# Ends of two feed-forward blocks reordered, and two half outputs of the next stage made before the stage boundary

## The chip, the cores and the metric

The kernel runs on one core of a Trainium2 chip. The metric is the device time of one execution in microseconds (us), taken as the median of several runs. The engines of the core work beside each other and wait for one another through semaphores: TensorE (PE in the rows: matmuls and transposes), VectorE (DVE), ScalarE (ACT), GpSimd (POOL), and SyncE (SP), which here issues the DMAs. A row "PE clock" gives the TensorE clock that was granted, as a share of its full 2.4 GHz; 0.50 is the lower of its two levels, 1.2 GHz.

## The reference

The computation is a two-layer encoder on 1024 tokens of width 1024, in float32. Layer 0 mixes with an S5 state space, layer 1 with an HGRN2 recurrence; after each mixer and after each feed-forward part a residual is added and a layer norm taken.

```python
def swiglu(x, w_in, w_out):
    gate, up = jnp.split(x @ w_in, 2, axis=-1)
    return (jax.nn.silu(gate) * up) @ w_out

def hgrn2_mixer(x, w_in, lower_bound, norm_g, w_out):
    q, f_fw, f_bw, i_in, g = jnp.split(x @ w_in, 5, axis=-1)   # width 1024 each
    ...                                   # q = silu(q); gates from f_fw, f_bw; 8 heads of 128
    o = rms_norm(o, norm_g) * jax.nn.silu(g)
    return o @ w_out

for layer in range(2):
    m = s5_mixer(h, ...) if layer == 0 else hgrn2_mixer(h, ...)
    h = layer_norm(ALPHA * h + m, ln_mix_g[layer], ln_mix_b[layer])
    f = swiglu(h, ffn_w_in[layer], ffn_w_out[layer])
    h = layer_norm(ALPHA * h + f, ln_ffn_g[layer], ln_ffn_b[layer])
```

## The kernel before, in words

The program is a row of stages, each an instruction block with a barrier of all engines at its end: S5, then `project_and_feed` (tiles named s5o), then the HGRN (tiles named hg), then `project_and_feed` again (tiles named hgo). The order of the instructions on each engine is the order in which each engine's own code is written; there is no scheduler. Each engine runs its list in order, and a wait at the head of the list holds up everything behind it.

**Numbers as pairs.** A float32 product is made of three matmuls of rounded parts: hi times hi, hi times lo, lo times hi. ScalarE makes a hi part (`split_hi`, line 62), VectorE or GpSimd subtracts it to get the lo part. The activations, with the width on the partitions, are `x_hi` and `x_lo` (tiles aT_hi, aT_lo).

**The feed-forward part.** The hidden width of 2816 is 22 chunks of 128, taken in 11 groups of two. For each group the two chunks are made, and `outputs` (lines 513 to 527) multiplies them with the group's rows of w_out: 16 products m = 0..15, two halves of the width for each of the eight token tiles, six matmuls each, into PSUM banks 4 + m % 4. VectorE adds each into h (`accumulate`, line 894). Bank m % 4 is free for product m + 4 once that is done (semaphore out_acc).

**The end of the last group (LAST), which the change touches.** The last chunk is made in a plain way in two token halves: `last_unit(0)` (four `plain_part`s of twelve matmuls, line 488, banks 0 and 1) and `last_unit(1)` (banks 2 and 3). Each half then passes ScalarE (silu), VectorE (`half_product`, line 875), ScalarE (hi) and GpSimd (`hidden_lo`, line 1023, semaphore hid) before `outputs` may use it. Tiles 0 to 3 need only half 0, tiles 4 to 7 need half 1. On TensorE the order is: last_unit(0), outputs of tiles 0 to 3, last_unit(1), transposes of tiles 0 to 3 (`turn_last`, line 411), outputs of tiles 4 to 7, transposes of tiles 4 to 7. The transposes put the normalised tokens into `x_hi` and `x_lo` for the HGRN, so they are there only in the first of the two blocks (`turns`); they go through the same banks 4 to 7, two banks a tile, and ScalarE and VectorE (`keep_turned`, line 831) empty them. After the second block the normalised rows go to the output.

VectorE takes the tiles in pairs. For each pair: `accumulate` with statistics (lines 894 and 897, two instructions for each product), then `normalise`: a chain of thirteen tiny instructions (lines 787 to 801) and four passes over 1024 columns (lines 805 and 808). `half_product` of half 1 stands behind pairs 0 and 1, then come keep_turned of tiles 0 to 3, then pairs 2 and 3, then keep_turned of tiles 4 to 7.

**The start of the HGRN.** For each head five outputs o = 0..4 (q, two forget gates, input, output gate) are made in two token halves: `unit(m, o, half)`, 24 matmuls at line 2112, into bank `half`. For head 0 all ten stand at the front of TensorE's list. A unit may overwrite its bank only when the result before it is read: unit (1, half) waits for q_kept, units (2, half) for f_kept. ScalarE starts with two small sigmoids of a table that depends on four DMAs of constants issued at the start of the stage, and only then takes the sigmoid of q (line 2246); VectorE then multiplies it (`keep_q`, line 2364). The weights of o = 0 and 1 of head 0 were already loaded and split in the block in front (w_raw, w_hi, w_lo); those of o = 2 are loaded at the start of the stage and split there when the units of o = 0, which share their buffer, are done.

## Time and profile before

| | us |
|---|---|
| median of 3 runs | 2784.15 |
| lowest, highest | 2781.75, 2785.19 |
| the profiled execution | 2782.6 |
| its span in the trace | 2780.8 |

TensorE is busy for 2562.8 us of that span, VectorE for 1831.1, GpSimd for 827.1, ScalarE for 813.5. The mean granted clock of TensorE is 0.959. The s5o block ends, and the HGRN begins, at about 1249.8 us of the span; the hgo block ends the program at 2780.8.

In a row of the timeline the first number is the start in us, the second the time from there to the end of the merged instructions, then engine, line, operation, what is written and read, the count, and in brackets the time the engine was idle before it and what ended that. One matmul of 512 columns shows about 0.39 us although the next starts sooner, since they overlap in the engine: the distance between starts is what counts.

### The profile page before, as it was taken

How to read it: one execution, taken by the hardware profiler on the slowest of the kernel's cores; microseconds unless marked ns; L12 is line 12 of the kernel's file. 1: busy time of each engine (PE TensorE's matmuls, PEld its weight loads, DVE VectorE, ACT ScalarE, POOL GpSimd, SP SyncE). 2: the span in 40 equal slices, each digit the busy share in tenths (PEclk: the TensorE clock that was granted, in tenths of full speed). 3: DMA queues.
4: the chain of work that ended last, by engine and by line, in shares of the span. 5: the costliest groups of instructions: out<-in, count | busy, mean ns of one | idle time of the engine just before them, and what ended most of it. 6: DMA issues, size and time to landing. Idle time of an engine off the chain costs nothing. (4 is left out here: it accounts for less than half of the span.)

```text
span 2780.8 us, 40502 instructions
## 1 busy us (share of the span) xinstructions
PE 2562.8 (92%) x13124; PEld 2148.0 (77%) x13124; DVE 1831.1 (66%) x3173; ACT 813.5 (29%) x1379; POOL 827.1 (30%) x606
## 2 busy tenths in 40 slices
PE   6787799999999999968999999997899999999995
PEld 5676577778888888757888888886687888888884
DVE  8789618666666666582667666667676666666657
ACT  3223323433332323312222323221233233323220
POOL 2968410433332323401111111110034333333240
PEclk9888899999999999989999999998899999999997
DMA  4333214134434434312010111000413444344341
GB/s 135 92 100 100 81 29 166 54 99 137 126 114 116 132 106 136 114 62 59 23 39 23 38 30 38 23 23 0 167 42 103 123 134 121 113 122 127 106 129 61
DMA packets 388063, 246.16 MB, mean 89 GB/s; under 512 B 23936, under 2 KB 370176, under 8 KB 387072
## 3 DMA queue, kind: packets, MB, share of 16 engines
q1 hardware_dynamic: 387968, 244.92, 29.5%
q8 instruction: 56, 0.92, 0.1%
q14 instruction: 39, 0.32, 0.0%
HBM read 227.10 MB, written 17.76 MB: 88 GB/s over the span
## 5 line engine op out<-in xcount | busy, mean ns | idle before, releaser
L894 DVE TENSOR_TENSOR h<-h,ps 128x512 f32<-128x512 f32 x320 | 219.1, 686 | 157.2 <-PE ps L525 157.0
L2112 PE MATMUL ps<-aT_hi,w_hi 128*128 128x512 f32 x640 | 257.1, 402 | 1.8 <-PEq L322 1.8
L2084 POOL TENSOR_TENSOR w_lo<-w_raw_plain,w_hi 128x1024 fp32r<-128x1024 f32 x38 | 91.8, 2423 | 560.1 <-ACT w_hi L62 560.1
L2112 PE MATMUL ps<-aT_hi,w_lo 128*128 128x512 f32 x640 | 251.5, 393 | 0.0
L2112 PE MATMUL ps<-aT_lo,w_hi 128*128 128x512 f32 x640 | 250.2, 391 | 0.0
L996 POOL TENSOR_TENSOR s5o_w_sets_plain<-s5o_w_sets_plain 128x512 f32<-128x512 f32 x100 | 137.4, 1379 | 223.8 <-DMA s5o_w_sets_plain<-in_ffn_w_in_dram 223.8
L476 PE MATMUL ps<-aT_hi,s5o_w_sets 128*128 128x512 f32 x640 | 203.0, 393 | 0.0
L476 PE MATMUL ps<-aT_hi,hgo_w_sets 128*128 128x512 f32 x640 | 202.8, 393 | 0.0
L996 POOL TENSOR_TENSOR hgo_w_sets_plain<-hgo_w_sets_plain 128x512 f32<-128x512 f32 x100 | 136.2, 1366 | 222.5 <-DMA hgo_w_sets_plain<-in_ffn_w_in_dram 222.4
L525 PE MATMUL ps<-hgo_w_hi,hgo_hid_hi 128*128 128x512 f32 x352 | 138.9, 395 | 11.6 <-POOL hgo_hid_lo L1023 11.6
L62 ACT ACTIVATE s5o_w_sets<-s5o_w_sets_plain 128x512 fp32r<-128x512 f32 x152 | 92.6, 627 | 178.7 <-POOL s5o_w_sets_plain L996 157.1
L62 ACT ACTIVATE hgo_w_sets<-hgo_w_sets_plain 128x512 fp32r<-128x512 f32 x152 | 92.7, 627 | 176.1 <-POOL hgo_w_sets_plain L996 155.9
L525 PE MATMUL ps<-s5o_w_hi,s5o_hid_hi 128*128 128x512 f32 x352 | 137.7, 391 | 5.1 <-POOL s5o_hid_lo L1023 3.4
L476 PEld LDWEIGHTS ps<-aT_hi,s5o_w_sets 128*128 128x128 f32 x640 | 120.5, 188 | 26.4
L2112 PEld LDWEIGHTS ps<-aT_hi,w_lo 128*128 128x128 f32 x640 | 120.3, 188 | 26.3
L476 PEld LDWEIGHTS ps<-aT_hi,hgo_w_sets 128*128 128x128 f32 x640 | 120.2, 188 | 26.3
L2112 PEld LDWEIGHTS ps<-aT_hi,w_hi 128*128 128x128 f32 x640 | 120.7, 189 | 25.0 <-issue 2.0
L2112 PEld LDWEIGHTS ps<-aT_lo,w_hi 128*128 128x128 f32 x640 | 120.6, 189 | 24.4
L525 PE MATMUL ps<-hgo_w_lo,hgo_hid_hi 128*128 128x512 f32 x352 | 138.4, 393 | 0.0
L525 PE MATMUL ps<-hgo_w_hi,hgo_hid_lo 128*128 128x512 f32 x352 | 138.4, 393 | 0.0
L525 PE MATMUL ps<-s5o_w_hi,s5o_hid_lo 128*128 128x512 f32 x352 | 137.7, 391 | 0.0
L525 PE MATMUL ps<-s5o_w_lo,s5o_hid_hi 128*128 128x512 f32 x352 | 137.6, 391 | 0.0
(380 smaller groups left out, 6332.3 us busy)
## 6 DMA issues: line engine op xcount, KB each, us to landing
s5o_w_sets_plain<-in_ffn_w_in_dram SPq DMA_DIRECT2D x208, 256.0 KB, 3.3
hgo_w_sets_plain<-in_ffn_w_in_dram SPq DMA_DIRECT2D x208, 256.0 KB, 3.3
w_raw_plain<-in_hg_w_in_dram SPq DMA_DIRECT2D x40, 512.0 KB, 4.0
s5o_w_sets_plain<-in_ffn_w_in_dram SPq DMA_DIRECT2D x96, 128.0 KB, 2.6
hgo_w_sets_plain<-in_ffn_w_in_dram SPq DMA_DIRECT2D x96, 128.0 KB, 2.7
s5o_w_lo_plain<-in_ffn_w_out_dram SPq DMA_DIRECT2D x11, 1024.0 KB, 5.0
hgo_w_lo_plain<-in_ffn_w_out_dram SPq DMA_DIRECT2D x11, 1024.0 KB, 5.0
h<-in_x_dram SPq DMA_DIRECT2D x4, 1024.0 KB, 8.9
```

What stands on the lines that cost most here:

```text
L62: return eng.activation(hi, src, ACT.Copy)
L476: ins = t.matmul(ps[:, to, :], w[:, kk, :], x_sets[x][xs][:, kk, :], start=(kk == 0 and m == 0), stop=(kk == 3 and m == 2))
L525: ins = t.matmul(ps[:, 4 + m % 4, :], x[:, q, tt * P:(tt + 1) * P], w[:, q, dh * HALF:(dh + 1) * HALF], start=(q == 0 and n == 0), stop=(q ...
L894: v.tensor_tensor(to, to, ps[:, 4 + m % 4, :], ALU.add).then_inc(S["out_acc"], 1)
L996: g.tensor_tensor(other, one, other, PRODUCTS[r][2]).then_inc(S["set_sum"], 1)
L2084: g.tensor_tensor(w_lo[b][:, :, :], w_raw[b][:, :, :], w_hi[b][:, :, :].bitcast(F32), ALU.subtract).then_inc(E[f"w_lo_done{b}"], 1)
L2112: ins = t.matmul(ps[:, half, :], w[b][:, kk, :], x[:, kk, cols], start=(kk == 0 and q == 0), stop=(kk == KT - 1 and q == 2))
```

## The change

Four things change.

1. On TensorE, in both feed-forward blocks, the first plain part of half 1 moves in front of the outputs of tiles 0 to 2, the other three stand behind them, and the outputs of tile 3 follow. The parts of half 1 wait for just the weight sets they need.
2. Tiles 4 to 7 are made in two pairs, each with the transposes of an earlier pair in front of it: transposes of 0 and 1, outputs of 4 and 5, transposes of 2 and 3, outputs of 6 and 7. The waits follow: a transpose of tile n waits until its two banks have been accumulated, and the outputs of tile t wait only for keep_turned of tile t - 4.
3. On VectorE `normalise` is cut in two (`moments`, the chain of tiny instructions, and `scale`, the four passes), half_product of half 1 moves in front of the scaling of pair 1, and keep_turned of tiles 2 and 3 stands between moments and scale of pair 2.
4. `next_units`: the units (0, half 0) and (1, half 0) of head 0 of the HGRN, 48 matmuls on the columns of tokens 0 to 511, are issued at the end of the s5o block, between the outputs of tiles 6 and 7 and the transposes of tiles 4 to 7, into banks 0 and 2. The HGRN's TensorE list starts with unit (0, half 1), then (1, half 1) and on; ScalarE reads the result of (1, half 0) from bank 2 and no longer waits for the two units that are there from the start.

```diff
@@ turn_last @@
                 t.wait_ge(S["normed"], NT + n + 1)
-                if n >= 2:
+                if n < 6:
+                    t.wait_ge(S["out_acc"], LAST * NOUT + 2 * (n + 3))
+                else:
                     t.wait_ge(S["hi"], NT + 2 * (n - 1))
                     t.wait_ge(S["lo"], NT + 2 * (n - 1))
@@ plain_part @@
-                t.wait_ge(S["plain_lo"], 6 * last + (n + 1 if half == 0 else 6))
+                t.wait_ge(S["plain_lo"], 6 * last + (n + 1 if half == 0 else (4, 4, 5, 6)[n]))
@@ tensor @@
+            def next_units():
+
+                t.wait_ge(S["next_lo"], 1)
+                t.wait_ge(S["hi"], NT + 2 * 4)
+                t.wait_ge(S["lo"], NT + 2 * 4)
+                t.wait_ge(S["half_silu"], 4)
+                t.wait_ge(S["half_product"], 4)
+                for o in range(2):
+                    hi, lo = (a[:, o * D:(o + 1) * D].rearrange("p (k n) -> p k n", k=KT) for a in (k.hi0, k.lo0))
+                    for kk in range(KT):
+                        for m, (w, x) in enumerate(((hi, x_hi), (hi, x_lo), (lo, x_hi))):
+                            t.matmul(ps[:, 2 * o, :], w[:, kk, :], x[:, kk, 0:HALF],
+                                     start=(kk == 0 and m == 0), stop=(kk == KT - 1 and m == 2))
@@ outputs @@
-                    if turns and isinstance(i, int) and i == LAST and m == NT:
-                        t.wait_ge(S["hi"], NT + 2 * 4)
-                        t.wait_ge(S["lo"], NT + 2 * 4)
+                    if turns and isinstance(i, int) and i == LAST and m >= NT and dh == 0:
+                        t.wait_ge(S["hi"], NT + 2 * (tt - 3))
+                        t.wait_ge(S["lo"], NT + 2 * (tt - 3))
@@ tensor, the end @@
-            last_unit(0)
-            outputs(LAST, slice(0, 4), 3)
-            last_unit(1)
+            t.wait_ge(S["merged"], (NF_LAST - 1) * NMERGE)
+            for n in range(4):
+                plain_part(True, 0, n)
+            plain_part(True, 1, 0)
+            outputs(LAST, slice(0, 3), 3)
+            for n in range(1, 4):
+                plain_part(True, 1, n)
+            outputs(LAST, slice(3, 4), 3)
+            for two in range(2):
+                if turns:
+                    turn_last(2 * two)
+                    turn_last(2 * two + 1)
+                outputs(LAST, slice(4 + 2 * two, 6 + 2 * two), 4)
             if turns:
-                t.wait_ge(S["out_acc"], LAST * NOUT + 8)
-                for n in range(4):
-                    turn_last(n)
-            outputs(LAST, slice(4, NT), 4)
+                next_units()
             if turns:
-                t.wait_ge(S["out_acc"], NG * NOUT)
                 for n in range(4, NT):
                     turn_last(n)
@@ vector, the end (normalise is now moments and then scale) @@
-            for pair in range(2):
-                accumulate(LAST, slice(2 * pair, 2 * pair + 2), last=True)
-                normalise((2 * pair, 2 * pair + 1), 2 * NT + 4 * pair + 4, 2, 2 * pair)
+            accumulate(LAST, slice(0, 2), last=True)
+            moments((0, 1), 2 * NT + 4)
+            scale((0, 1), 2, 0)
+            accumulate(LAST, slice(2, 4), last=True)
+            moments((2, 3), 2 * NT + 8)
             half_product(True, 1)
+            scale((2, 3), 2, 2)
...
@@ the HGRN @@
+    def unit_bank(m, o, half):
+
+        return 2 * o if first(m) and o < 2 and half == 0 else half
...
-                ins.then_inc(E["unit_done"], 1)
+                ins.then_inc(E["unit_done"], 2 if first(m) and o < 2 else 1)
...
             for u in range(2 * OUTS):
-                unit(0, u // 2, u % 2)
+                if unit_bank(0, u // 2, u % 2) == u % 2 and u:
+                    unit(0, u // 2, u % 2)
```

On VectorE, at the end of the s5o block, this stands before at the end of the moments of tiles 2 and 3 (L805 and L808 are the passes of normalise, L875 is half_product, L831 keep_turned, L894 and L897 accumulate):

```order
L801 SCALAR_TENSOR_TENSOR s5o_rstd<-s5o_tmp,s5o_rstd 128x2 [waits s5o_chain]
L805 SCALAR_TENSOR_TENSOR h<-h,s5o_mv,s5o_x_plain 128x1024 [waits s5o_rows,s5o_chain]
...
L808 SCALAR_TENSOR_TENSOR h<-h,s5o_rstd,s5o_x_plain 128x1024 [waits s5o_scaled]
L875 TENSOR_TENSOR s5o_act_out<-s5o_act_out,ps 128x512 [waits s5o_half_silu]
L831 TENSOR_TENSOR aT_lo<-ps,aT_hi 128x4x128 [waits s5o_hi] x8
L894 TENSOR_TENSOR h<-h,ps 128x512 [waits s5o_out_tile]
L897 BN_STATS stats<-h 128x6 [waits s5o_out_acc]
```

and this stands there now (L825 and L828 are scale, L899 is half_product, L855 keep_turned, L918 and L921 accumulate):

```order
L818 SCALAR_TENSOR_TENSOR s5o_rstd<-s5o_tmp,s5o_rstd 128x2 [waits s5o_chain]
L899 TENSOR_TENSOR s5o_act_out<-s5o_act_out,ps 128x512 [waits s5o_half_silu,s5o_chain]
L825 SCALAR_TENSOR_TENSOR h<-h,s5o_mv,s5o_x_plain 128x1024 [waits s5o_rows]
...
L828 SCALAR_TENSOR_TENSOR h<-h,s5o_rstd,s5o_x_plain 128x1024 [waits s5o_scaled]
L855 TENSOR_TENSOR aT_lo<-ps,aT_hi 128x4x128 [waits s5o_hi] x4
L918 TENSOR_TENSOR h<-h,ps 128x512 [waits s5o_out_tile]
...
L818 SCALAR_TENSOR_TENSOR s5o_rstd<-s5o_tmp,s5o_rstd 128x2 [waits s5o_chain]
L855 TENSOR_TENSOR aT_lo<-ps,aT_hi 128x4x128 [waits s5o_hi,s5o_chain]
L855 TENSOR_TENSOR aT_lo<-ps,aT_hi 128x4x128 [waits s5o_hi] x3
L825 SCALAR_TENSOR_TENSOR h<-h,s5o_mv,s5o_x_plain 128x1024 [waits s5o_rows]
```

Half_product has moved in front of the four passes, and four of the eight keep_turned instructions have moved behind the accumulation of tiles 4 and 5 and their moments.

On TensorE, from the end of the outputs of tiles 6 and 7 in the s5o block to the barrier, before (L525 is outputs, L411 a transpose):

```order
L525 MATMUL ps<-s5o_w_hi,s5o_hid_hi 128x512 [waits s5o_out_acc]
...
L411 MATMUL ps<-ident,h 128x128 [waits s5o_hi,s5o_lo,s5o_normed,s5o_out_acc]
L411 MATMUL ps<-ident,h 128x128 x7
L411 MATMUL ps<-ident,h 128x128 [waits s5o_lo,s5o_hi,s5o_normed]
...
L411 MATMUL ps<-ident,h 128x128 x7
L322 UNCONDITIONAL_BRANCH
L2093 UNCONDITIONAL_BRANCH [waits barrier_Pool_Activation_PE_DVE_SP_release]
```

and now (L536 is outputs, L521 is next_units):

```order
L536 MATMUL ps<-s5o_w_hi,s5o_hid_hi 128x512 [waits s5o_out_acc]
...
L521 MATMUL ps<-aT_hi,w_hi 128x512 [waits s5o_half_silu,s5o_lo,s5o_half_product,s5o_hi,s5o_next_lo]
L521 MATMUL ps<-aT_lo,w_hi 128x512
L521 MATMUL ps<-aT_hi,w_lo 128x512
...
L411 MATMUL ps<-ident,h 128x128 [waits s5o_out_acc,s5o_normed]
L411 MATMUL ps<-ident,h 128x128 x7
L411 MATMUL ps<-ident,h 128x128 [waits s5o_out_acc,s5o_normed]
L411 MATMUL ps<-ident,h 128x128 x7
L411 MATMUL ps<-ident,h 128x128 [waits s5o_lo,s5o_hi,s5o_normed]
```

The 48 matmuls of next_units (only their first three are shown) stand in front of the first transpose of tile 4, and the transposes of tiles 4 and 5 no longer wait for hi and lo.

## Rows read from the trace of the kernel before

**Rows 1.** The page, busy time of each engine (share of the span) and instructions.

```profile
PE 2562.8 (92%) x13124; PEld 2148.0 (77%) x13124; DVE 1831.1 (66%) x3173; ACT 813.5 (29%) x1379; POOL 827.1 (30%) x606
```

**Rows 2.** Stretches: length, busy time of each engine, PE clock, DMA share, GB/s.

```profile
1215.60:1226.70 11.10, 11.02 (x48) 8.93 (x48) 8.74 (x22) 0.00 (x0) 0.00 (x0) 1.00 0.01 1
...
1226.70:1235.00 8.30, 0.14 (x1) 0.00 (x0) 8.16 (x10) 0.00 (x0) 0.00 (x0) 0.73 0.31 126
```

**Rows 3.** Timeline of TensorE, end of the s5o block and start of the HGRN.

```profile
1178.24 0.50 PE L525 MATMUL ps<-s5o_w_hi,s5o_hid_hi 128*128 128x512 f32 x1 [3.42 <-POOL s5o_hid_lo L1023]
...
1180.88 0.63 PE L525 MATMUL ps<-s5o_w_hi,s5o_hid_lo 128*128 128x512 f32 x1
...
1181.31 0.63 PE L525 MATMUL ps<-s5o_w_hi,s5o_hid_hi 128*128 128x512 f32 x1
...
1201.84 1.91 PE L411 MATMUL ps<-ident,h 128*128 128x128 f32 x16
...
1210.78 3.25 PE L411 MATMUL ps<-ident,h 128*128 128x128 f32 x16 [7.03 <-ACT aT_hi L62]
...
1215.68 0.47 PE L525 MATMUL ps<-s5o_w_hi,s5o_hid_hi 128*128 128x512 f32 x1 [1.65 <-DVE aT_lo L831]
...
1235.10 3.68 PE L411 MATMUL ps<-ident,h 128*128 128x128 f32 x16 [8.26 <-DVE h L894]
...
1244.76 3.32 PE L411 MATMUL ps<-ident,h 128*128 128x128 f32 x16 [5.98 <-DVE aT_lo L831]
...
1249.83 0.47 PE L2112 MATMUL ps<-aT_hi,w_hi 128*128 128x512 f32 x1 [1.75 <-PEq L322]
```

**Rows 4.** Timeline of VectorE, end of the s5o block.

```profile
1180.34 0.69 DVE L894 TENSOR_TENSOR h<-h,ps 128x512 f32<-128x512 f32 x1 [4.16 <-PE ps L525]
...
1194.57 0.68 DVE L894 TENSOR_TENSOR h<-h,ps 128x512 f32<-128x512 f32 x1
...
1199.96 0.28 DVE L787 BATCH_NORM_AGGREGATE s5o_mv<-stats 128x2 f32<-128x12 f32 x2
...
1202.44 1.29 DVE L805 SCALAR_TENSOR_TENSOR h<-h,s5o_mv,s5o_x_plain 128x1024 f32<-128x1024 f32 x1
...
1207.48 0.68 DVE L875 TENSOR_TENSOR s5o_act_out<-s5o_act_out,ps 128x512 f32<-128x512 f32 x1
...
1217.34 0.69 DVE L894 TENSOR_TENSOR h<-h,ps 128x512 f32<-128x512 f32 x1 [1.81 <-PE ps L525]
...
1243.33 2.48 DVE L831 TENSOR_TENSOR aT_lo<-ps,aT_hi 128x512 fp32r<-128x512 f32 x4
```

**Rows 5.** Timeline of VectorE, ScalarE, then SyncE, first work of the HGRN.

```profile
1255.90 0.17 DVE L2356 TENSOR_TENSOR hg_lb_diff<-hg_lb_in 128x8 f32<-128x8 f32 x1 [6.39 <-DMA hg_norm_g<-in_hg_norm_g_dram]
1257.07 0.69 DVE L2364 TENSOR_TENSOR hg_q_raw<-hg_sigmoid,ps 128x512 f32<-128x512 f32 x1 [1.00 <-ACT hg_sigmoid L2246]
1256.44 0.60 ACT L2246 ACTIVATE hg_sigmoid<-ps 128x512 f32<-128x512 f32 x1
1253.33 63.16 SPq L2069 DMA_DIRECT2D w_raw_plain<-in_hg_w_in_dram  x7
```

**Rows 6.** The page: GpSimd's split of weights, then a load to landing (us).

```profile
L2084 POOL TENSOR_TENSOR w_lo<-w_raw_plain,w_hi 128x1024 fp32r<-128x1024 f32 x38 | 91.8, 2423 | 560.1 <-ACT w_hi L62 560.1
...
w_raw_plain<-in_hg_w_in_dram SPq DMA_DIRECT2D x40, 512.0 KB, 4.0
```

**Rows 7.** Timeline of TensorE, then of VectorE, end of the hgo block.

```profile
2715.78 0.80 PE L525 MATMUL ps<-hgo_w_hi,hgo_hid_hi 128*128 128x512 f32 x1 [3.41 <-POOL hgo_hid_lo L1023]
...
2747.57 0.80 PE L525 MATMUL ps<-hgo_w_hi,hgo_hid_hi 128*128 128x512 f32 x1 [8.23 <-POOL hgo_hid_lo L1023]
...
2744.84 0.68 DVE L875 TENSOR_TENSOR hgo_act_out<-hgo_act_out,ps 128x512 f32<-128x512 f32 x1
...
2750.54 0.69 DVE L894 TENSOR_TENSOR h<-h,ps 128x512 f32<-128x512 f32 x1 [5.02 <-PE ps L525]
...
2753.08 0.69 DVE L894 TENSOR_TENSOR h<-h,ps 128x512 f32<-128x512 f32 x1 [1.12 <-PE ps L525]
```

47 lines of the change are left out of this document (29 added, 18 removed).

## The prediction

> **What bounds the kernel now.** I read the page first: TensorE is busy for 92% of the span [rows 1], so the ends of blocks, where it waits, are what an order can win. Then TensorE's timeline there with the engine that ended each wait, then VectorE's beside it, and the stretches for the clock.
>
> At the end of the s5o block TensorE waits five times: 3.42 us for half 0's hidden part (GpSimd's, last of silu, product, hi, lo), 7.03 and 1.65 us around the transposes of tiles 2 and 3, 8.26 us for tile 4's normalised rows, 5.98 us for VectorE's keep_turned [rows 3]. In the stretch of 8.3 us in which TensorE does nothing VectorE is busy for 8.16 [rows 2]. So VectorE's list sets the end: from moments of pair 1 at 1199.96 to keep_turned of tile 4 at 1243.33 [rows 4] are 43.37 us. TensorE's first HGRN matmul starts 6.5 us after that, at 1249.83 [rows 3], behind keep_turned of tiles 4 and 5 and the transposes of 6 and 7. From there TensorE sets the pace: ten units back to back. At the end of the hgo block VectorE again is last, after a wait of 5.02 us [rows 7].
>
> **Prices.** At full clock (1.00, that is 2.4 GHz) 48 matmuls take 11.0 us, 0.229 each [rows 2]; at the lower level, 1.2 GHz, the starts are 0.43 apart (1180.88, 1181.31 [rows 3]), 0.20 more each. A unit of 24 is 5.5 us, a plain part or a tile's outputs (12) 2.75. VectorE: moments 2.48 (1199.96 to 1202.44), scale of a pair 5.04 (1202.44 to 1207.48), four keep_turned 2.48, a pair's accumulation without waits 5.39 (1194.57 to 1199.96), half_product 0.70 [rows 4]. The first accumulation follows its outputs' start by 1.66 us at full clock [rows 3, 4], by 2.97 us at the lower one, and the second is then 1.12 us late as well [rows 7].
>
> **Part 1, the plain part in the gap.** Half 0's chain is untouched, so the outputs still start at 1178.24 (s5o) and 2715.78 (hgo). 2.75 us of the 3.4 are filled, and an idle of about 0.7 is left. Behind the 3.4 us the clock fell for a while in both blocks [rows 3, 7]; behind 0.7 us I expect it not to, since it was up behind 1.65 and 1.75 us [rows 2, 3]. Both ends:
> - Clock stays up. The first accumulation comes 1.66 instead of 2.10 us after the start (1180.34 [rows 4]) and those behind it gain more. But product 6 now stands behind 36 + 36 + 6 matmuls: 78 x 0.228 + 0.3 = 18.1 us after the start, 1196.35, and product 7 1.36 later; VectorE ends the accumulation of pair 1 at 1199.1. That is 0.85 earlier in s5o, 0.7 in hgo by the same sum.
> - Clock falls as before. With 6.5 to 8 slow matmuls 1.3 to 1.6 us are added to product 6: 0.75 later in s5o, 0.65 in hgo.
>
> I take the first.
>
> **Parts 2 and 3, s5o from there to the scaled tiles 6 and 7.** VectorE's new list: moments 3 x 2.48, product 0.70, scale 3 x 5.04, keep_turned 2 x 2.48, accumulation 2 x 5.39 = 39.0 us; the same instructions as before, so the gain is in the waits, 4.3 us of the 43.37. Now: half_product starts at 1199.1 + 2.5 = 1201.6, half 1 of the hidden part is there 2.7 later (in hgo 2744.84 to 2747.57 [rows 7]), early. TensorE waits instead for keep_turned of tile 0, behind scale: 1202.3 + 5.04 + 1.24 = 1208.6, an idle of over 9 us. Behind idles of 7 and 8.3 us TensorE ran at the lower level (transposes 3.25 and 3.68 instead of 1.91 [rows 3]; first accumulation at 2.97 [rows 7]), so VectorE, 1.24 us into the other keep_turned, waits 2.97 - 1.24 = 1.7, and 1.1 for the next product. Nothing later waits: the outputs of 4 and 5 take 12 x 0.43 + 12 x 0.23 = 7.9 us to 1216.6, the transposes of 2 and 3 end at about 1219, before moments of pair 2 end (1208.6 + 2.97 + 5.39 + 1.1 + 2.48, about 1221); the outputs of 6 and 7 start behind one keep_turned at 1222 and are there before scale of pair 2 ends (1228). Sum 39.0 + 2.8 + 0.1 = 41.9 against 43.37: 1.4 us, with part 1 2.2. At full clock the waits would be 0.4: 4.7. At the lower end 1.4 - 0.75 = 0.65.
>
> **Part 4, next_units in s5o.** Outputs of 6 start at 1222 behind an idle of 3 us, end at 1229 with part of them at the lower level, next_units end at 1240.2, the transposes of 4 and 5 at 1242. VectorE is through with scale at 1241.1 to 1241.3 and needs the first of them then: cover about nil, a cost of 0 to 0.5. If the lower clock reaches 8 more matmuls it is 1.6. Against that, the transposes of 6 and 7 come right behind dense work: 1.91 instead of 3.32 us [rows 3], VectorE's end 1.1 us earlier. Net +0.6, between -1.6 and +1.1. The 48 matmuls write banks 0 and 2, which nobody reads by then. GpSimd's and SP's lists are the same; the HGRN's first loads are issued behind the barrier as before.
>
> **Part 4, the start of the HGRN.** Two of ten units go: 11.0 us. A wait comes. Unit (0, half 1) is done 5.5 us after the start, and (1, half 1) needs its bank read, q_kept twice. ScalarE's first sigmoid does not start before the constants: VectorE's lb_diff at 1255.90 is ended by norm_g's DMA, the sigmoid of q is at 1256.44, the product at 1257.07 [rows 5], all hidden today beside unit (0, half 1). Now sigmoid of half 1 follows at once, its product ends at about 1257.07 + 2 x 0.69 = 1258.45, 8.65 us after the start. Idle 8.65 - 5.5 = 3.15 us. Queued behind it are all the other units, so nothing fills it. Behind 3.42 and 3.41 us the clock fell at a cost of 1.3 to 1.6 us; I take 1.5, between none and 1.6. The next units are safe: f_kept of half 0 comes from bank 2, and the weights of o = 2 are loaded at +3.5 (1253.33 [rows 5]), 4.0 us to landing and 2.4 for GpSimd's split [rows 6], with 1.2 for ScalarE's (1024 columns at 0.60 for 512 [rows 5]): +11.1, wanted at +14.2. Gain 11.0 - 3.15 - 1.5 = 6.35, 7.9 if the clock stays.
>
> **Part 3 in hgo.** From the end of pair 1's accumulation to tile 4's before: 2.48 + 5.04 + 0.70 + 5.02 = 13.25. Now moments, half_product, then scale beside the hidden part: 8.24, and the outputs start 2.73 after half_product's start, their first result 2.97 later, 5.70, as scale ends (5.74). So 5.0, with part 1 5.7 (4.35 at the low end; 6.9 at full clock, without the 1.12). All that follows is VectorE's list in the same order, without waits, and the last store.
>
> **Sum.** 2.2 + 0.6 + 6.35 + 5.7 = 14.85 us off the profiled execution of 2782.6, whose span is 2780.8: 2767.8. That execution lies 1.5 below the median of 2784.15, inside the runs' spread of 3.4; taken from the median it is 2769.3. I say **2769**. Least from the bounds: 0.65 - 1.6 + 6.35 + 4.35 = 9.75, 2774.4; most: 4.7 + 1.1 + 7.9 + 6.9 = 20.6, 2763.6.
>
> **Rivals.**
> - *The weights take the wait over.* w_raw of o = 2 is loaded behind the constants, and the units that hid load, ScalarE's and GpSimd's split are two fewer. The margin is 3.1 us [rows 5, 6]. A load that lands 6 us late, among the constants and the other weights, costs 3: 2772.
> - *Transposes too late.* If all 72 matmuls from outputs 6 to next_units run at the lower level they end at 1222 + 31 = 1253, and the block ends near 1263 (3.7 for the transposes of 4 and 5, 6.5 for the rest), 13 us later than now instead of 2.8 earlier. 6.35 + 5.7 - 13 is about -1: 2784 to 2785, no change. If only half do, 7 us are lost and 2776 remains. For it: tiny bursts with waits stand in front. Against: the outputs at 1215.68 ran at full clock two waits after an idle of 7 us [rows 2, 3].
> - *Slower.* One mechanism: the lower level holds from the outputs of tile 6 through next_units, the transposes and the first HGRN units. Each matmul there costs 0.20 us, and VectorE's cover is gone. The block's end loses 13 as above, and HGRN units at the lower level 4.8 us each; with four of them 19: 2784 + 19 - 1.5 = 2801. It decides from the second such unit on. Against it: the first of today's units starts at full clock 1.75 us behind slow transposes [rows 3].
>  This is also what the Trainium skill would have one fear: "TensorE: Matmul & The Clock Gate", section "A second HAM failure mode: psum-queue depth-cycling", says that short idles between groups of matmuls can make the clock swing between its levels, so that throughput goes to the swings. The change does cut two long waits into more short ones. By that rule the time would be that of this rival; by the rows above it is not, since 1.65 and 1.75 us did not bring the clock down.
> - *Nothing moves.* The order on the engines is changed as said, so this could only be the second rival.
>
> **How the numbers follow.** Forecast 0.74; weights 0.08; late transposes 0.12 (half of it at no change, half at 2776); slower 0.04; 0.02 for what I don't see, on either side. A change of 0.2%, 5.6 us, is about what a measurement can tell here. Faster 0.74 + 0.08 + 0.06 + 0.01 = 0.89, same 0.06, slower 0.05. The range 2763 to 2777 takes in both bounds and the milder rivals.
>
> **What would show it.** After: the first outputs of both ends at 1178.2 and behind an idle under 1 us, clock 1.00 after; pair 1's accumulation ending near 1199; tile 4's outputs near 1208.7 at the lower level; next_units from 1229 in 11 us; the HGRN's first matmul near 1247; there an idle of 3 us behind 24 matmuls, ended by the product of q, then seven units without a wait; tile 4's accumulation of hgo 5.7 us earlier by its own block's time. It is wrong if the weights end a wait, if next_units take over 15 us, or if VectorE waits between 1220 and 1243.

## The result, and the profile after

The changed kernel takes 2765.67 us (median of five runs, 2762.03 to 2769.28) where the kernel before takes 2784.15 (median of five, one of which took 6893 us and counts for nothing in the ratio): a ratio of 0.9934, 95% interval [0.9923, 0.9946]. That is 18.5 us less, of which the forecast had 14.85. The profiled execution took 2762.03 us, with a span of 2760.2; before, 2782.6 and 2780.8. Its engines are as busy as before within 0.3%; TensorE's share rises because nearly the same busy time fills a shorter span [rows 1]:

```profile
PE 2555.6 (93%) x13124; PEld 2141.2 (78%) x13124; DVE 1832.3 (66%) x3173; ACT 811.4 (29%) x1379; POOL 828.1 (30%) x606
```

To say where the time went I cut each trace at the same four events. A is the end of the s5o block, from the first matmul of half 0's outputs to the first matmul of the HGRN. B runs from there to the first matmul of the HGRN's diagonal. "Mid" is the untouched rest up to hgo's outputs, and C the stretch from there to the end of the span.

| | start of A | A | B | mid | C |
|---|---|---|---|---|---|
| before | 1178.24 | 71.59 | 63.91 | 1402.04 | 65.02 |
| changed | 1174.53 | 69.03 | 55.13 | 1402.43 | 59.08 |
| gain | 3.71 | 2.56 | 8.78 | -0.39 | 5.94 |

The five gains are the 20.6 us between the two spans. The first of them can't be told from chance: ahead of A the change touches only what TensorE does in the idle gap, and in the 14 traces of this case, whose kernels are otherwise alike up to there, the start of A lies anywhere from 1174.4 to 1180.7. In a second trace of the changed kernel it is 1177.9, with A 68.91, B 55.15 and C 59.12. So I put 17.3 us down to the change, at three places, and read them in turn.

Timeline of TensorE in the changed kernel (start, duration, engine, line, operation, operands; in brackets the idle time before it and what ended it), with the plain part in the gap and next_units at the end:

```profile
1174.53 0.50 PE L536 MATMUL ps<-s5o_w_hi,s5o_hid_hi 128*128 128x512 f32 x1 [0.68 <-POOL s5o_hid_lo L1058]
...
1205.91 0.77 PE L536 MATMUL ps<-s5o_w_hi,s5o_hid_hi 128*128 128x512 f32 x1 [9.98 <-DVE aT_lo L855]
...
1218.57 0.47 PE L536 MATMUL ps<-s5o_w_hi,s5o_hid_hi 128*128 128x512 f32 x1 [3.47 <-DVE aT_lo L855]
...
1239.45 2.26 PE L411 MATMUL ps<-ident,h 128*128 128x128 f32 x16 [0.79 <-ACT aT_hi L62]
...
1243.56 0.47 PE L2151 MATMUL ps<-aT_hi,w_hi 128*128 128x512 f32 x1 [1.84 <-PEq L322]
...
1251.22 0.50 PE L2151 MATMUL ps<-aT_hi,w_hi 128*128 128x512 f32 x1 [1.92 <-DVE hg_q_raw L2407]
...
2701.12 0.50 PE L536 MATMUL ps<-hgo_w_hi,hgo_hid_hi 128*128 128x512 f32 x1 [0.67 <-POOL hgo_hid_lo L1058]
...
2727.61 0.79 PE L536 MATMUL ps<-hgo_w_hi,hgo_hid_hi 128*128 128x512 f32 x1 [7.03 <-POOL hgo_hid_lo L1058]
```

The five waits of the s5o end [rows 3] were 3.42, 7.03, 1.65, 8.26 and 5.98 us. Now the first is 0.68; then comes one long one of 9.98, ended by VectorE's keep_turned, one of 3.47 and one of 0.79. Then there is a new wait, inside the HGRN: 1.92 us behind the first unit, ended by VectorE's product of q. Where the clock stood is in the stretches (length, busy time of PE, PEld, DVE, ACT, POOL, granted clock of PE, DMA share, GB/s):

```profile
1196.00:1205.90 9.90, 0.00 (x0) 0.02 (x1) 9.48 (x18) 2.58 (x5) 1.58 (x1) 0.65 0.18 74
1205.90:1209.00 3.10, 3.09 (x7) 2.46 (x8) 1.21 (x3) 0.00 (x0) 0.00 (x0) 0.50 0.28 107
...
1218.50:1222.00 3.50, 3.43 (x10) 2.76 (x11) 3.46 (x4) 0.00 (x0) 0.00 (x0) 0.63 0.00 0
...
1230.00:1236.00 6.00, 6.00 (x28) 4.93 (x27) 5.55 (x16) 0.00 (x0) 0.00 (x0) 1.00 0.02 10
1249.30:1251.20 1.90, 0.00 (x1) 0.00 (x0) 1.29 (x2) 1.04 (x2) 0.00 (x0) 1.00 1.14 327
1251.20:1257.00 5.80, 5.78 (x25) 4.78 (x26) 0.00 (x0) 2.03 (x3) 2.40 (x1) 1.00 0.28 74
```

Behind 9.98 us of idle the outputs of tile 4 run at 0.50, the lower level (1.2 GHz). Behind 3.47 us the outputs of tile 6 start at full clock, but 0.8 us later the clock falls, and it is 0.50 from 1219.4 to 1222.8: eight matmuls start 0.43 us apart, and the 0.63 is the mean of that stretch. No engine waits for them here (VectorE's 1224.56 has no wait). next_units run at 1.00, and the clock is still 1.00 behind the new wait of 1.92 us. The length of the first row behind a wait (0.47 or 0.50 at full clock, about 0.77 at the lower level) tells where the clock stood at that matmul and not where it stood a microsecond later, so each case needs the rows behind it too. In the first stretch VectorE works through nearly all of TensorE's idle time: it is still VectorE's list that sets the block's end. That list, and then the one instruction of GpSimd that lies beside it:

```profile
1195.48 0.28 DVE L804 BATCH_NORM_AGGREGATE s5o_mv<-stats 128x2 f32<-128x12 f32 x2
...
1199.88 2.17 DVE L828 SCALAR_TENSOR_TENSOR h<-h,s5o_rstd,s5o_x_plain 128x1024 f32<-128x1024 f32 x1
1201.97 1.27 DVE L825 SCALAR_TENSOR_TENSOR h<-h,s5o_mv,s5o_x_plain 128x1024 f32<-128x1024 f32 x1
...
1204.48 2.48 DVE L855 TENSOR_TENSOR aT_lo<-ps,aT_hi 128x512 fp32r<-128x512 f32 x4
...
1208.84 0.69 DVE L918 TENSOR_TENSOR h<-h,ps 128x512 f32<-128x512 f32 x1 [1.89 <-PE ps L536]
...
1210.45 0.69 DVE L918 TENSOR_TENSOR h<-h,ps 128x512 f32<-128x512 f32 x1 [0.20 <-PE ps L536]
...
1224.56 0.68 DVE L918 TENSOR_TENSOR h<-h,ps 128x512 f32<-128x512 f32 x1
...
1238.02 2.48 DVE L855 TENSOR_TENSOR aT_lo<-ps,aT_hi 128x512 fp32r<-128x512 f32 x4 [0.46 <-ACT aT_hi L62]
...
1248.71 0.17 DVE L2399 TENSOR_TENSOR hg_lb_diff<-hg_lb_in 128x8 f32<-128x8 f32 x1 [5.48 <-DMA hg_norm_g<-in_hg_norm_g_dram]
...
1249.88 1.29 DVE L2407 TENSOR_TENSOR hg_q_raw<-hg_sigmoid,ps 128x512 f32<-128x512 f32 x2 [1.00 <-ACT hg_sigmoid L2287]
...
2724.55 0.69 DVE L899 TENSOR_TENSOR hgo_act_out<-hgo_act_out,ps 128x512 f32<-128x512 f32 x1
...
2726.47 2.17 DVE L828 SCALAR_TENSOR_TENSOR h<-h,hgo_rstd,hgo_x_plain 128x1024 f32<-128x1024 f32 x1
...
2731.07 0.68 DVE L918 TENSOR_TENSOR h<-h,ps 128x512 f32<-128x512 f32 x1
```

```profile
1199.39 1.58 POOL L1058 TENSOR_TENSOR s5o_hid_lo<-s5o_act_out,s5o_hid_hi 128x512 fp32r<-128x512 f32 x1 [19.77 <-ACT s5o_hid_hi L62]
```

The reader sees the new list (moments, half_product, scale, keep_turned, accumulation) with waits of 1.89, 0.20 and 0.46 us where there were 43.37 us with 4.3 of waits. One pass of scale is longer than its like: 2.17 us where the next takes 1.27. It lies beside GpSimd's hidden_lo, which takes 1.58. The same stands in hgo (2726.47). There the wait of 5.02 us [rows 7] is gone: 2731.07 follows without one. In the HGRN VectorE takes the difference of the constants (hg_lb_diff), as soon as they have landed, 5.15 us after the first matmul (6.07 before [rows 3, 5]), and both products of q go back to back in 1.29 us.

### The profile page after: what moved, and what is told of

Its sections match the earlier page's. It is cut to its first block and busy times, and to the rows that moved or that the text cites. A ratio compares the mean times of both kernels' runs of the same rounds, so it can differ in the third digit from the quotient of the medians.

```text
span 2760.2 us, 40508 instructions
## 1 busy us (share of the span) xinstructions
PE 2555.6 (93%) x13124; PEld 2141.2 (78%) x13124; DVE 1832.3 (66%) x3173; ACT 811.4 (29%) x1379; POOL 828.1 (30%) x606
## 5 line engine op out<-in xcount | busy, mean ns | idle before, releaser
L918 DVE TENSOR_TENSOR h<-h,ps 128x512 f32<-128x512 f32 x320 | 219.0, 685 | 149.8 <-PE ps L536 149.4
L2151 PE MATMUL ps<-aT_hi,w_hi 128*128 128x512 f32 x624 | 250.9, 402 | 3.8 <-DVE hg_q_raw L2407 1.9
L2151 PE MATMUL ps<-aT_hi,w_lo 128*128 128x512 f32 x624 | 245.3, 393 | 0.0
L2151 PE MATMUL ps<-aT_lo,w_hi 128*128 128x512 f32 x624 | 244.4, 392 | 0.0
L536 PE MATMUL ps<-s5o_w_hi,s5o_hid_hi 128*128 128x512 f32 x352 | 138.7, 394 | 14.1 <-DVE aT_lo L855 13.4
L62 ACT ACTIVATE s5o_w_sets<-s5o_w_sets_plain 128x512 fp32r<-128x512 f32 x152 | 92.6, 627 | 178.6 <-POOL s5o_w_sets_plain L1031 156.8
L536 PE MATMUL ps<-hgo_w_hi,hgo_hid_hi 128*128 128x512 f32 x352 | 138.0, 392 | 7.7 <-POOL hgo_hid_lo L1058 7.7
L536 PE MATMUL ps<-s5o_w_lo,s5o_hid_hi 128*128 128x512 f32 x352 | 138.2, 393 | 0.0
L536 PE MATMUL ps<-s5o_w_hi,s5o_hid_lo 128*128 128x512 f32 x352 | 138.0, 392 | 0.0
L536 PE MATMUL ps<-hgo_w_lo,hgo_hid_hi 128*128 128x512 f32 x352 | 137.6, 391 | 0.0
L536 PE MATMUL ps<-hgo_w_hi,hgo_hid_lo 128*128 128x512 f32 x352 | 137.6, 391 | 0.0
L2187 PE MATMUL ps<-hg_q_decayed,hg_k_used 128*128 128x128 f32 x896 | 125.2, 297 | 13.0 <-DVE hg_q_decayed L2475 12.4
L862 DVE TENSOR_TENSOR hgo_w_sets<-hgo_w_sets_plain,hgo_w_sets 128x512 fp32r<-128x512 f32 x140 | 129.8, 945 | 11.1 <-ACT hgo_w_sets L62 10.6
```

The source lines that it names most:

```text
L62: return eng.activation(hi, src, ACT.Copy)
L536: ins = t.matmul(ps[:, 4 + m % 4, :], x[:, q, tt * P:(tt + 1) * P], w[:, q, dh * HALF:(dh + 1) * HALF], start=(q == 0 and n == 0), stop=(q ...
L862: v.tensor_tensor(lo, plain_rows(pos)[1], hi.bitcast(F32), ALU.subtract).then_inc(S["set_lo"], 1)
L918: v.tensor_tensor(to, to, ps[:, 4 + m % 4, :], ALU.add).then_inc(S["out_acc"], 1)
L2151: ins = t.matmul(ps[:, half, :], w[b][:, kk, :], x[:, kk, cols], start=(kk == 0 and q == 0), stop=(kk == KT - 1 and q == 2))
L2187: ins = t.matmul(bank_rows(2 + 2 * (lv % 2))[:, c, :], k_used[lv % 2][:, c * HC:(c + 1) * HC], q_used(lv, c), start=True, stop=True)
```

## Experiments

Two theories stood against each other. **Theory 1** is the prediction's: VectorE's list sets A and C, the wait for q's products sets B, and the clock follows from how long TensorE idled. The first two held; the third held only in part, as the runs below show. **Theory 2** is the rival: that part of the gain, or of what is missing from it, comes from somewhere else (contention, the weights, chance in the clock). Which of these a run is about, its expectation says. All twelve runs, with the kernel before run on the same chip:

| kernel | median us (runs) | before | ratio [95%] | A | B | C |
|---|---|---|---|---|---|---|
| changed, again | 2764.74 (5) | 2784.07 | 0.9933 [0.9920, 0.9947] | 68.91 | 55.15 | 59.12 |
| no next_units | 2774.90 (6) | 2784.07 | 0.9968 [0.9955, 0.9980] | 70.78 | 66.64 | 59.22 |
| next_units only | 2779.23 (11) | 2784.07 | 0.9982 [0.9973, 0.9991] | 73.69 | 60.40 | 65.29 |
| gap open | 2770.17 (5) | 2784.07 | 0.9947 [0.9933, 0.9960] | 72.01 | 56.19 | 59.77 |
| keep first | 2763.30 (5) | 2783.30 | 0.9932 [0.9919, 0.9946] | 65.75 | 55.36 | 59.04 |
| bank 3 | 2764.25 (5) | 2783.30 | 0.9933 [0.9920, 0.9947] | 68.92 | 53.73 | 59.27 |
| lo on VectorE | 2769.03 (5) | 2783.30 | 0.9945 [0.9932, 0.9959] | 68.78 | 58.32 | 58.94 |
| q first | 2767.85 (5) | 2783.30 | 0.9942 [0.9928, 0.9956] | 68.96 | 54.63 | 59.23 |
| together | 2762.36 (5) | 2782.52 | 0.9923 [0.9910, 0.9937] | 65.73 | 53.88 | 59.00 |
| constants late | 2772.38 (5) | 2782.52 | 0.9963 [0.9950, 0.9977] | 71.17 | 61.40 | 59.37 |
| next_units only, again | 2778.20 (11) | 2782.52 | 0.9988 [0.9979, 0.9997] | 73.67 | 56.97 | 65.30 |
| next_units and q first | 2777.23 (7) | 2782.52 | 0.9969 [0.9958, 0.9980] | 73.72 | 54.61 | 65.22 |

A, B and C come from one execution each, the times from all runs; an interval of a ratio is some 5 to 7.5 us wide, so what is under 3 us shows only in the stretches.

### The two halves of the change

The changed kernel once more, as the measure for the others:

> The changed kernel once more, on the chip of the next three, as their base. Three lengths are read in every trace: A, in the s5o block from the first matmul of the outputs of half 0 to the HGRN's first matmul (71.59 us before, 69.03 in the changed kernel's trace); B, from there to the first matmul of the HGRN's diagonal (63.91, 55.13); C, in the hgo block from the first matmul of the outputs of half 0 to the end of the span (65.02, 59.10). All theories expect A 69.0, B 55.1, C 59.1 within 0.3 us, since nothing is changed. If the 3.7 us by which the trace already led at the start of A come from the change, they are there again; if they are the state of the clock in the S5 stage of one execution, they are not.

Without next_units (the order alone):

```diff
-                next_units()
-            if turns:
...
-                if unit_bank(0, u // 2, u % 2) == u % 2 and u:
-                    unit(0, u // 2, u % 2)
+                unit(0, u // 2, u % 2)
```

> The changed kernel without next_units: all ten units of head 0 stand in the HGRN again, the order of the feed-forward blocks' ends stays. My theory (the early units are worth two units less a stall, and cost the block's end almost nothing): B back to 63.9, C 59.1, A 69.6, since VectorE's wait of 0.46 us for the transposes goes but the transposes of tiles 6 and 7 run at the lower clock again (about 1 us). In all 8.8 + 0.6 = 9.4 us slower than the changed kernel, about 2775. Rival (next_units hold the block's end up, the order alone would do): A under 67.5, total under 2773. Rival (the order of the s5o block gained only by the warmer clock): A 71.

And the kernel before with next_units alone (run twice, the second time with more executions):

```diff
             if turns:
+                next_units()
+            if turns:
                 t.wait_ge(S["out_acc"], NG * NOUT)
...
-                unit(0, u // 2, u % 2)
+                if unit_bank(0, u // 2, u % 2) == u % 2 and u:
+                    unit(0, u // 2, u % 2)
```

> The kernel before with next_units and the shorter start of the HGRN, placed behind the outputs of tiles 4 to 7; the old order of both feed-forward blocks' ends. My theory: the 48 matmuls fill the 8.3 us in which TensorE waited for tile 4 and some 3 us more, the transposes of 4 and 5 are still ahead of VectorE, and those of 6 and 7 run at full clock: A 70.5, B 55.1, C 65.0, 9.9 us faster than before, 2774. With the order alone (9.4 us slower than the changed kernel) the two sum up to the whole within 1 us. Rival (they need each other: without the new order next_units come too late): A 73 or more, 2777 or more.

> The kernel before with next_units alone, once more, for a second trace: the first gained 4.8 us where 9.9 were expected, with A 73.7 and B 60.4 in a trace of a slower execution. If these two lengths are what this kernel does, they come again within 1 us (theory 1: the long idles of the old order leave the clock low for the outputs and the last transposes, and the constants land late). If they are the luck of one execution (theory 2), A is nearer to 71 and B to 56 to 58, and the median stays at 2779 only through a mix.

The order alone gives 9.2 us (2784.07 to 2774.90), a little over the 7.9 of its terms. Its A and B were to be 69.6 and 63.9; they are 70.78 and 66.64, in a trace of the slowest of its six executions (2780.46, 5.6 us over their median). next_units alone give 4.8 and 4.3, about half of what was expected. Both together give 19.3: some 5 us more than the sum of the halves, which intervals of 5 to 7.5 us on each of the three don't separate from nothing.

In the new order A is 70.78 without next_units and 68.91 with them. In the old order it is 73.69, 73.67 and 73.72 with them (three traces), and 71.59 without (one trace). Neither difference is shown to be the work of next_units, since most of both arises ahead of them. In the old order VectorE waits 3.08 us and then 0.33 to 0.38 for tile 4's outputs in the three traces, where it waited once, for 1.81, before [rows 4], and the code is the same up to there; when VectorE comes to the wait for the transposes of tiles 6 and 7, which is where next_units can first tell, it is 1.9 of the 2.1 us late. In the new order the trace without next_units has the second wait for tile 4's outputs at 1.15 us, where the changed kernel has 0.20. A trace with next_units and that same 1.15 is below, and its A is 71.17, so between like and like next_units save nothing in A. TensorE's timeline of the order alone, ahead of the HGRN:

```profile
1242.65 3.65 PE L411 MATMUL ps<-ident,h 128*128 128x128 f32 x16 [8.51 <-DVE aT_lo L853]
...
1247.98 0.76 PE L2145 MATMUL ps<-aT_hi,w_hi 128*128 128x512 f32 x1 [1.68 <-PEq L322]
```

Without next_units TensorE stands for 8.51 us, and the transposes of tiles 6 and 7 take 3.65 us where the changed kernel's take 2.26. The first unit of the HGRN starts at the lower level here (0.76), which costs 1.6 us of B; the other 1.1 by which B is over before's are spread over the ten units, whose matmuls start 0.233 us apart in this trace and 0.229 in before's, at a granted clock of 1.00 in both.

TensorE's timeline with next_units in the old order, the first trace, then VectorE's wait for tile 4's outputs:

```profile
1218.25 0.77 PE L539 MATMUL ps<-s5o_w_hi,s5o_hid_hi 128*128 128x512 f32 x1 [1.50 <-DVE aT_lo L847]
...
1248.99 3.54 PE L411 MATMUL ps<-ident,h 128*128 128x128 f32 x16 [5.18 <-DVE aT_lo L847]
...
1263.78 0.80 PE L2132 MATMUL ps<-aT_hi,w_hi 128*128 128x512 f32 x1 [3.81 <-DVE hg_q_raw L2388]
```

```profile
1221.19 0.69 DVE L910 TENSOR_TENSOR h<-h,ps 128x512 f32<-128x512 f32 x1 [3.08 <-PE ps L539]
```

There VectorE is further behind, so TensorE is through with next_units and the transposes of tiles 4 and 5 5.18 us before it can start the last transposes, and these run slowly all the same (3.54). The outputs of tiles 4 to 7 start at the lower level (0.77), where before's trace has 0.47 [rows 3]. In the new order the idle time in front of the last transposes is only 0.79 us. B differs between the two traces of the same code, 60.40 and 56.97, while A came again within 0.02. The second trace, and in it the stretch that begins 0.8 us behind the wait:

```profile
1243.43 3.50 PE L411 MATMUL ps<-ident,h 128*128 128x128 f32 x16 [5.15 <-DVE aT_lo L847]
...
1256.53 0.50 PE L2132 MATMUL ps<-aT_hi,w_hi 128*128 128x512 f32 x1 [2.16 <-DVE hg_q_raw L2388]
```

```profile
1257.30:1260.70 3.40, 3.40 (x9) 2.63 (x8) 0.00 (x0) 0.85 (x2) 2.34 (x1) 0.51 0.01 2
```

The wait for q is 3.81 us with the clock at the lower level from the first matmul on (0.80), or 2.16 us with a fast first matmul (0.50) and the lower level from 0.8 us later. VectorE's timeline of the first trace says why the waits differ:

```profile
1261.27 0.17 DVE L2380 TENSOR_TENSOR hg_lb_diff<-hg_lb_in 128x8 f32<-128x8 f32 x1 [7.38 <-DMA hg_norm_g<-in_hg_norm_g_dram]
```

The constants landed 7.05 us after the first HGRN matmul there, against 5.40 in the second. That is 1.65 us of the 3.43 between the two B. Another 1.1 are the clock, which was at 0.50 for 6.8 us in the first (2.7 us of cost, by the trace of *constants late* below) and for 3.4 in the second (1.6). The last 0.7 are the spacing of the matmuls behind it, 0.234 us in the first trace, much as in that of the order alone, and 0.229 in the second.

### The gap and the contention

The plain part taken out of the gap again:

```diff
-            plain_part(True, 1, 0)
-            outputs(LAST, slice(0, 3), 3)
-            for n in range(1, 4):
+            outputs(LAST, slice(0, 4), 3)
+            for n in range(4):
```

> The changed kernel with its first edit undone: the outputs of tiles 0 to 3 directly behind half 0's parts, then all four parts of half 1. My theory: the idle before the first outputs is 3.4 us again and the clock falls behind it, but pair 1's accumulation is VectorE's own pace there as before, so it ends 0.8 us later, and half_product waits up to 0.6 us for the parts. A 69.8 to 70.4, C 59.9 to 60.5, B 55.1; 1.6 to 2.8 us slower than the changed kernel, about 2768. Rival (filling the gap is what gained, with its clock): C 63 or more and A 71 or more, 2774.

TensorE's timeline:

```profile
1179.22 0.59 PE L536 MATMUL ps<-s5o_w_hi,s5o_hid_hi 128*128 128x512 f32 x1 [3.42 <-POOL s5o_hid_lo L1056]
...
1211.68 0.76 PE L536 MATMUL ps<-s5o_w_hi,s5o_hid_hi 128*128 128x512 f32 x1 [6.94 <-DVE aT_lo L853]
...
1225.35 0.77 PE L536 MATMUL ps<-s5o_w_hi,s5o_hid_hi 128*128 128x512 f32 x1 [3.47 <-DVE aT_lo L853]
```

The wait of 3.42 us is back, and tile 4's outputs start 32.46 us into A instead of 31.38: 1.1 later, near the 0.85 of part 1. C is 0.65 longer (0.7 forecast). But A is 3.1 us longer and the median 5.4, more than I had expected; A is where the rival had it (71 or more), C isn't (63 or more). The rest is the clock. Tile 4's outputs have twelve slow starts here and seven in the changed kernel, so VectorE's second wait for them is 1.14 us and not 0.20, and its wait for the transposes of tile 4 is 1.35 and not 0.46: 0.9 us each. The HGRN's first unit is slow as well, for another 1.6 in B. Behind the same 3.47 or 3.48 us of idle the clock fell at tile 6's outputs in all ten traces of the new order. In seven of them it did so 0.3 to 1.0 us behind the first matmul (0.47) and stayed down for 3.4 us; in three (no next_units, gap open, constants late) it fell within the wait, so that the first matmul was slow already (0.76 or 0.77), and stayed down for 6.8 us, and these three are the ones with an A over 70 us. Whether an open gap makes that likelier, one trace can't tell. The median lies over the changed kernel's by more than part 1's terms, so it doesn't speak against them.

GpSimd's last subtraction given to VectorE, between the two passes of scale, in both blocks:

```diff
+            def last_lo():
+                v.wait_ge(S["hid_hi"], 2 * NF_LAST + 2)
+                v.tensor_tensor(hid_lo[:, 1, HALF_COLS[1]], act_out[1][:, :],
+                                hid_hi[:, 1, HALF_COLS[1]].bitcast(F32), ALU.subtract).then_inc(S["hid"], 1)
...
-            scale((2, 3), 2, 2)
+            scale((2, 3), 2, 2, last_lo)
...
-            hidden_lo(NF_LAST, 1, (1,))
```

> The changed kernel with the lo part of half 1's hidden values made by VectorE, between the first and the second pass of the scaling of pair 1, instead of by GpSimd beside them. Theory 1 (the pass at L828 took 2.17 instead of 1.28 us because GpSimd's two-input subtraction ran beside it, both engines reading SBUF): all four passes take 1.28, VectorE's list grows by one instruction of some 0.66 us, so A and C are 0.2 us shorter, about 68.7 and 58.9. Theory 2 (the pass was long for another reason, a wait inside it or the data): one pass is 2.17 still, A and C 0.7 longer.

VectorE's timeline:

```profile
1204.47 1.28 DVE L836 SCALAR_TENSOR_TENSOR h<-h,s5o_rstd,s5o_x_plain 128x1024 f32<-128x1024 f32 x1
...
1206.98 1.29 DVE L836 SCALAR_TENSOR_TENSOR h<-h,s5o_rstd,s5o_x_plain 128x1024 f32<-128x1024 f32 x1
```

With nothing on GpSimd beside them, the passes at L836 (L828 in the changed kernel) take 1.28 and 1.29 us. A is 68.78 (68.91) and C 58.94 (59.12), since the subtraction now costs VectorE about what the contention did. So the 0.9 us were contention. But B is 58.32 in this trace, and the median, 2769.03, is 3 to 4 us over the changed kernel's where it was to be 0.4 under. TensorE's and VectorE's timelines and a stretch show what B is made of:

```profile
1247.41 0.76 PE L2158 MATMUL ps<-aT_hi,w_hi 128*128 128x512 f32 x1 [1.85 <-PEq L322]
```

```profile
1254.14 0.17 DVE L2406 TENSOR_TENSOR hg_lb_diff<-hg_lb_in 128x8 f32<-128x8 f32 x1 [7.06 <-DMA hg_norm_g<-in_hg_norm_g_dram]
```

```profile
1257.60:1261.00 3.40, 3.40 (x10) 2.61 (x9) 0.00 (x0) 0.78 (x2) 2.26 (x1) 0.50 0.01 3
```

The first unit starts at the lower level behind 1.85 us and takes 7.3 us instead of 5.7. The constants land late, at +6.73, but beside the longer unit that leaves the wait at 1.93. Behind this wait the clock falls for 3.4 us, 1.0 us after the first matmul. The two falls are the 3.2 us of B, 1.6 each; neither is in the edit. What the other four executions of this kernel did no trace shows.

The Trainium skill has the rule for the contention ("SBUF — State Buffer", section "SBUF: two separate sides"): VectorE and GpSimd share one pair of ports, taken for a whole instruction, and a VectorE operation with two inputs in SBUF is blocked while a GpSimd operation that reads SBUF holds it. The trace agrees (2.17 against 1.28 us for a pass whose two inputs lie in SBUF), and in the next experiment the four keep_turned, with one input in PSUM, keep their 2.48 us.

keep_turned of tiles 0 and 1 put ahead of scale, so that it is they that lie beside GpSimd's subtraction, and the hi and lo parts that tile 4's outputs wait for are made earlier (on ScalarE its part of them moves in front of half 1's hi part):

```diff
-            scale((2, 3), 2, 2)
             if turns:
                 keep_turned(0)
                 keep_turned(1)
+            scale((2, 3), 2, 2)
```

> The changed kernel with keep_turned of tiles 0 and 1 moved once more: on VectorE in front of the scaling of pair 1, on ScalarE in front of half 1's hi part. Base: A 68.9, B 55.15, C 59.1 (changed kernel, twice). Theory 1 (in the s5o block VectorE's own list and its wait behind that keep_turned set the end): the outputs of tile 4 start some 26.3 us after those of tile 0 instead of 31.4, VectorE's wait of 1.89 us before them goes, and the pass at L828 that lies beside GpSimd's hidden_lo (2.17 instead of 1.28 us) is not beside it any more: A 66.1 to 66.4, B and C as before, 2.7 us faster than the changed kernel. Theory 2 (TensorE's list with next_units sets the end of the block): A stays at 68.5 to 69.

TensorE's and VectorE's timelines:

```profile
1203.26 0.80 PE L536 MATMUL ps<-s5o_w_hi,s5o_hid_hi 128*128 128x512 f32 x1 [4.79 <-POOL s5o_hid_lo L1061]
```

```profile
1201.11 2.48 DVE L858 TENSOR_TENSOR aT_lo<-ps,aT_hi 128x512 fp32r<-128x512 f32 x4
...
1204.82 1.28 DVE L831 SCALAR_TENSOR_TENSOR h<-h,s5o_rstd,s5o_x_plain 128x1024 f32<-128x1024 f32 x1
...
1208.54 0.68 DVE L921 TENSOR_TENSOR h<-h,ps 128x512 f32<-128x512 f32 x1
```

Tile 4's outputs start 26.2 us into A instead of 31.4, released by GpSimd, and VectorE no longer waits for them (1208.54 has no bracket). A is 65.75, 3.2 us shorter, even below the 66.1 to 66.4 expected: the waits of 1.89 and 0.20 and the 0.9 of contention are 3.0 of that. This is Theory 1 at its plainest: the same instructions on VectorE, and the waits between them gone. The median is only 1.4 to 2.4 us below the changed kernel's, which the intervals don't separate from none.

### The start of the HGRN

Where q's products are what is waited for, a third bank should take the wait away:

```diff
+        return 3 if first(m) and o == 1 else half
...
-                if o == 1:
+                if o == 1 and not first(m):
                     t.wait_ge(E["q_kept"], 2 * m + 1 + half)
+                if o == 2 and first(m):
+                    t.wait_ge(E["q_kept"], 1 + half)
```

> The changed kernel with unit (1, half 1) of head 0 put into bank 3, so that it does not wait until q's second half is read; the units of o = 2 wait for that instead. Theory 1 (the stall in the HGRN's start is the whole of what B lies above eight units): no wait behind the first unit, B 53.2 to 53.5. Theory 2, the rival of the prediction (the weights of o = 2 take the wait over, since in the changed kernel GpSimd ends their split 11.4 us after the start and two units end at 11.0): an idle of 0.4 to 1.5 us two units in, B 53.7 to 54.7. Which of the two, depends on how late the constants land, since ScalarE takes them first.

TensorE's timeline:

```profile
1257.81 0.50 PE L2155 MATMUL ps<-aT_hi,w_hi 128*128 128x512 f32 x1 [0.52 <-POOL w_lo L2125]
```

The wait of 1.91 us behind the first unit is gone, and one of 0.52 for GpSimd's split of the weights has taken its place two units in. B is 53.73 instead of 55.15. So the rival of the weights is real, at 0.5 us, but only once q's wait has gone; and q's wait, not the weights, held B in the changed kernel.

The same wait, shortened from the other side: q's sigmoids and products ahead of the constants.

```diff
+            s.dma_start(w_raw[0][:, :, :], w_v[:, 2, :, ds(0, P)]).then_inc(E["w_loaded0"], 16)
...
-            a.wait_ge(E["lb_chain"], 1)
-            a.activation(lb[:, 0, :], d_lb[:, :], ACT.Sigmoid).then_inc(E["lb_act"], 1)
...
-            v.wait_ge(E["consts"], 16 * 4)
-            v.tensor_tensor(d_lb[:, :], lb_in[:, 1, :], lb_in[:, 0, :], ALU.subtract).then_inc(E["lb_chain"], 1)
```

(The removed lines return behind q's.)

> The changed kernel with another order at the HGRN's start: the load of the weights of o = 2 is issued ahead of the constants, ScalarE takes both sigmoids of q ahead of the two that need the constants, VectorE both products of q ahead of lb_diff. Theory 1 (the stall's length is set by the landing of the constants, +5.2 us in the changed kernel, +6.1 before, +7.05 in the kernel with the next units alone, where the clock fell behind a stall of 3.8): the stall is now the first unit's end plus sigmoid and product, 1.3 to 1.6 us, whenever the constants land, the clock stays, B 54.5 to 54.8, and the runs spread less. Theory 2 (the stall is bound by something else, as the read of bank 1 itself): B 55.1 or more.

TensorE's timeline:

```profile
1256.77 0.50 PE L2152 MATMUL ps<-aT_hi,w_hi 128*128 128x512 f32 x1 [1.41 <-DVE hg_q_raw L2405]
```

The wait is 1.41 instead of 1.91 and B 0.5 shorter, as it should be when it no longer hangs on the constants. The time doesn't show it: the median is 2767.85, 2 to 3 us over the changed kernel's, and the five runs spread over 5.4 us, where they were to spread less. And the constants' DMAs put behind two loads of weights, to lengthen the wait:

```diff
-            s.dma_start(mask[:, :, :], masks.rearrange("l s t -> s l t")).then_inc(E["consts"], 16)
...
-            for o in range(2, OUTS):
+            for o in range(2, 4):
...
+            s.dma_start(mask[:, :, :], masks.rearrange("l s t -> s l t")).then_inc(E["consts"], 16)
```

> The changed kernel with the constants' four DMAs issued behind the first two loads of weights instead of ahead. Theory 1 (the landing of the constants sets the stall, and a stall of over 3 us brings the clock down): constants 2 us or more later, +7.5 to +9.5, a wait behind the first unit of 4.3 to 6.5 us, the clock at its lower level behind it for 1 to 2 us of cost, B 58.5 to 62, 4 to 6 us slower than the changed kernel in the total. Theory 2 (the stall's length has another cause): B 55 to 56.

TensorE's timeline, then VectorE's, then the stretch behind the wait:

```profile
1219.66 0.77 PE L536 MATMUL ps<-s5o_w_hi,s5o_hid_hi 128*128 128x512 f32 x1 [3.47 <-DVE aT_lo L855]
...
1256.81 0.80 PE L2152 MATMUL ps<-aT_hi,w_hi 128*128 128x512 f32 x1 [3.87 <-DVE hg_q_raw L2408]
```

```profile
1240.07 2.48 DVE L855 TENSOR_TENSOR aT_lo<-ps,aT_hi 128x512 fp32r<-128x512 f32 x4 [1.41 <-ACT aT_hi L62]
...
1254.30 0.17 DVE L2400 TENSOR_TENSOR hg_lb_diff<-hg_lb_in 128x8 f32<-128x8 f32 x1 [9.02 <-DMA hg_norm_g<-in_hg_norm_g_dram]
```

```profile
1256.80:1260.00 3.20, 3.19 (x8) 2.51 (x9) 0.00 (x0) 1.05 (x3) 2.39 (x1) 0.50 0.00 0
```

The constants land at +8.69, the wait is 3.87 us, and the clock behind it is 0.50. B is 61.40: 6.3 longer, of which 1.95 are the wait and 4.3 the clock, 2.7 here and 1.6 at the first unit. The wait is shorter than the 4.3 to 6.5 us that were expected, because the slow first unit covers 1.6 us of it.

With this run a sum can be put to the test. VectorE's difference of the constants is followed by the sigmoids and the two products of q, and TensorE goes on 2.5 us after the difference starts; it stands from its first unit's end until then. So the wait is the constants' landing plus 2.5 less the length of the first unit: 5.15 + 2.5 - 5.75 = 1.9 in the changed kernel, 7.05 + 2.5 - 5.75 = 3.8 with next_units alone, 5.40 + 2.5 - 5.75 = 2.15 in its second trace, 6.73 + 2.5 - 7.3 = 1.9 with lo on VectorE, 6.21 + 2.5 - 7.3 = 1.4 with the gap open, 8.69 + 2.5 - 7.3 = 3.9 here. Measured are 1.92, 3.81, 2.16, 1.93, 1.43 and 3.87.

The trace shows something else as well: with the code of the s5o end unchanged, the clock is down from the first matmul of tile 6's outputs, as with the gap open (0.77 behind 3.47 us), VectorE's second wait for tile 4's outputs is 1.15 us and its wait for the transposes of tile 4 1.41, and A is 71.17. The late transposes, a rival of the prediction, are 0.95 of the 2.2 us by which A is longer, the second wait another 0.95. This came in one of the six traces that have this code (lo on VectorE counted among them).

Last, does q first mend the next_units in the old order?

```diff
+            s.dma_start(w_raw[0][:, :, :], w_v[:, 2, :, ds(0, P)]).then_inc(E["w_loaded0"], 16)
...
-            for o in range(2, OUTS):
+            for o in range(3, OUTS):
```

(on next_units only, with the moves of q first on ScalarE and VectorE)

> The kernel before with next_units, and q and the weights ahead of the constants. If the stall of 3.8 us and the lower clock behind it are where the gain of the early units went, the stall is 1.4 us now, the clock stays, B is 54.6 to 55.0 and the median 3 to 5 us below that of next_units alone (2779), 2774 to 2776. Rival (the gain was lost in the s5o block's end): B as said, but the median within 2 us of 2779.

TensorE's timeline:

```profile
1261.49 0.50 PE L2133 MATMUL ps<-aT_hi,w_hi 128*128 128x512 f32 x1 [1.41 <-DVE hg_q_raw L2386]
```

The wait is 1.41 again and B 54.61, 2.4 and 5.8 us below its two sisters; C is as before. The median is 1 to 2 us below theirs, as the rival has it; but its seven runs spread over 9.4 us, and its ratio's interval hardly touches that of the second next_units only, so 3 to 5 us aren't excluded. What next_units alone still fail to give in this trace lies in the block's end, at 73.7 us of A, most of it ahead of next_units, as said.

### The best of them together

Keep first, bank 3 and q first, and GpSimd's subtraction on VectorE in the hgo block alone:

```diff
+        return 3 if first(m) and o == 1 else half
...
                 keep_turned(0)
                 keep_turned(1)
+            scale((2, 3), 2, 2, None if turns else last_lo)
```

> The changed kernel with four edits of the runs before together: keep_turned of tiles 0 and 1 ahead of the scaling, unit (1, half 1) in bank 3, weights and q ahead of the constants, and in the hgo block alone the lo part of half 1 on VectorE. By my account of the single runs A is 65.75, as with the first alone; B 53.2, since no wait is left in the start (the weights' 0.52 us goes with their earlier load); C 58.9. That is 3.2 + 1.9 + 0.2 = 5.3 us faster than the changed kernel, about 2760. Rival (the single runs' traces don't add up, since TensorE's list with next_units becomes the bound of the block's end): A 67 or more, 2763.

TensorE's timeline:

```profile
1257.20 0.50 PE L2168 MATMUL ps<-aT_hi,w_hi 128*128 128x512 f32 x1 [0.68 <-POOL w_lo L2138]
```

Its ratio of 0.9923 [0.9910, 0.9937] is the lowest of all, 2762.36 us, and its three stretches are 178.6 us together where the changed kernel's are 183.2. The interval overlaps with that of the changed kernel, so that it beats it stands on the stretches. B was to be 53.2 and is 53.88: 0.68 us for the weights remain. I left ScalarE's two sigmoids of the constants ahead of its split of those weights, and the constants, now issued behind a load, land at +7.79; the split starts at +8.33.

## Why the prediction was right, point by point

**Part 1 held.** The outputs start behind 0.68 us (0.7 forecast) in s5o and 0.67 in hgo. Pair 1's accumulation ends 20.95 us into A, where the sum gave 20.86 and before had 21.72. The clock stayed up.

**Parts 2 and 3 in s5o held in sum, by two errors that cancel.** Tile 4's outputs start at +31.38, not at +30.4, because the pass beside GpSimd took 2.17 us; I had priced every pass at its undisturbed time. Against that VectorE waited 1.89 and 0.20 us, not 1.7 and 1.1. Pair 3 is scaled at +63.0, forecast +62.9 to +63.1.

**next_units in s5o held.** They cost VectorE 0.46 us (0 to 0.5 forecast), and the transposes of tiles 6 and 7 take 2.26 us instead of 3.32. (The 0.46, at 1238.02, is by the letter one of the signs of being wrong, a wait of VectorE between 1220 and 1243; the sum had already allowed for it.) Tile 6's outputs ran in part at the lower level, as forecast. A gained 2.56, forecast 2.8.

**The start of the HGRN is the term that was mis-sized.** I forecast 11.0 - 3.15 - 1.5 = 6.35 and B gained 8.78 in the one trace and 8.76 in the other. The wait came, at its place and ended by what I had named, but it was 1.92 us: the constants landed at +5.15 where before's trace has +6.07, which is 0.9 of the difference of 1.2, and the first unit takes 5.7 us to its end and not 5.5. Behind 1.92 us the clock stayed, so the 1.5 weren't paid either. That was in part luck: in two other traces about that 1.5 was paid behind waits of the same size (1.6 us behind 1.93 and 2.16). The upper end of 7.9 left the wait at 3.15; it should have let the landing move too, which lies from +5.15 to +7.05 in the traces that leave its code alone. Where it came late (+7.05, +8.69), the wait was 3.81 and 3.87 and the clock fell for longer: the mechanism was right and one trace's landing was not its size.

**hgo held in sum, by two errors that cancel as well.** C gained 5.94, forecast 5.7. From the end of pair 1's accumulation to tile 4's are 9.0 us, not 8.24, since the pass beside GpSimd is longer here too. Against that the wait of 1.12 us for the next product [rows 7], which the 5.7 left standing, is gone: the outputs start 3.06 us after half_product, and no wait of VectorE stands behind them.

**The rivals.** The weights never ended a wait in the changed kernel; they did for 0.5 us once the wait for q was taken away. Late transposes came in one of six traces, for about 1 us and not for 7 or 13. The rival *Slower*, with the lower level from tile 6's outputs through to the HGRN units, was in no trace. The sum of the terms is 2.4 us short in B and right within 0.3 elsewhere; with the 17.3 us the changed kernel would stand at 2766.9 from the median of before, against 2765.67 and 2764.74 measured.

**What stays open.** How often the kernel before has the short A of its single trace (71.59). Whether the two halves of the change are worth more together than apart. And why the same waits with the same code leave the clock up in some traces and down in others: in front of the HGRN (1.7 to 1.85 us) up in ten and down in four.

## What to carry to other kernels

When an engine's list sets the end, count its instructions once and then only its waits: what an order can win is those waits, and the next one to come is found by asking what is ready last. Work that fills another engine's idle time can also keep the clock up for what follows it, if little idle time lies between: in these traces the last transposes took 2.26 us with 0.79 us of idle in front of them, 3.50 to 3.54 with 5.2 us and the same 48 matmuls ahead, and 3.65 behind 8.5 us without next_units. (By the medians the 48 matmuls gave 4 to 5 us in the old order and 10 in the new, but the intervals don't separate the two.) Price a new wait on a DMA with the spread of its landing over several traces, and a two-input pass beside GpSimd with the contention.

## What the runs showed of the hardware

- The clock is not a function of the last idle time, and it can fall after work has started again. Behind 0.67 to 0.69 us in front of the outputs it never fell (nine traces, both blocks). Behind 1.41 to 2.16 us inside the HGRN it fell in two of eight traces (behind 1.93 and 2.16), 0.8 and 1.0 us after the first matmul and for 3.4 us; behind 1.91, 1.92 and 2.15 it stayed up. In the waits of 3.81 and 3.87 us it fell before the first matmul, for 6.8 us both times, at a cost of 2.7. At tile 6's outputs, behind 3.47 us, it fell in all ten traces of the new order, for 3.4 us in seven and for 6.8 in three. At the HGRN's start, behind 1.7 to 1.85 us, it was down in four of fourteen, at a cost of 1.6 us in B each time (in one of the four it had been down since before the last transposes).
- Four DMAs of constants (one of 448 KB, two of 4 KB and one of 0.5 KB) landed from 5.15 to 7.05 us after the same event, for the same code.
- The same 1175 us of work ahead of A differed by 6.2 us between executions, more than most edits here moved. In two traces of fourteen the matmuls of the HGRN's first units started 0.233 and 0.234 us apart, in the others 0.228 or 0.229, all at a granted clock of 1.00.
- VectorE's pass and GpSimd's subtraction, each with two inputs in SBUF, slow each other: 2.17 and 1.58 us together, 1.28 and 1.27 apart. keep_turned, with one input in PSUM, doesn't: 2.48 for four and 1.26 together.
